# The mean of squares in front of four norms: eight matmul pairs each, or a sum on VectorE and two

## What is computed

```
def rms_norm(x, g):
    xf = x.astype(jnp.float32)
    y = xf * lax.rsqrt(jnp.mean(xf * xf, axis=-1, keepdims=True) + NORM_EPS)
    return (y * g.astype(jnp.float32)).astype(x.dtype)
...
h = h + rms_norm(mixed, W['g_post_mix'][l])
f = rms_norm(h, W['g_pre_ffn'][l]) @ W['w_ffn_in'][l]
f = (jax.nn.silu(f[..., :D_FF]) * f[..., D_FF:]) @ W['w_ffn_out'][l]
h = h + rms_norm(f, W['g_post_ffn'][l])
```

## Time and profile before

| | us |
|---|---|
| median of three runs | 1995.92 |
| the three runs | 1991.81, 1995.92, 2005.24 |
| profiled execution | 2002.46 |
| its span, first to last instruction | 2000.7 |
| TensorE matmul busy | 1829.9 |
| VectorE busy | 790.2 |
| ScalarE busy | 604.3 |
| mean granted clock of TensorE, share of full | 0.954 |

### The profile page before, as it was taken

The page is one execution under the profiler, slowest core; times in us unless marked ns, Lnnn a source line. Parts: engine busy times, 40 slices in busy tenths (PEclk is TensorE's granted clock), DMA queues, the critical chain, the costliest instruction groups (busy, mean ns, idle before and its releaser), DMA issues.

```text
span 2000.7 us, 39700 instructions
## 1 busy us (share of the span) xinstructions
PE 1829.9 (91%) x18348; PEld 1677.0 (84%) x18348; DVE 790.2 (39%) x1122; ACT 604.3 (30%) x992; POOL 22.4 (1%) x37
## 2 busy tenths in 40 slices
PE   7999999879779899999999899677778999999995
PEld 6677789869769799999999799465538999999995
DVE  1556224455541454224432543525123444144422
ACT  4224034323252422122212421344535322222112
POOL 0000000010000000000000000100000000000000
PEclk9999999989969999999999899878988999999998
DMA  8221130001033153464413221241835222333211
GB/s 276 67 80 61 42 96 5 4 16 43 28 117 115 57 184 128 145 224 152 139 59 103 102 92 46 96 139 42 205 80 163 64 78 59 107 85 85 62 55 48
DMA packets 208821, 187.53 MB, mean 94 GB/s; under 512 B 13976, under 2 KB 199448, under 8 KB 207504
## 3 DMA queue, kind: packets, MB, share of 16 engines
q1 hardware_dynamic: 205440, 170.74, 28.0%
q0 software_dynamic: 3216, 14.26, 2.0%
HBM read 170.72 MB, written 41.13 MB: 106 GB/s over the span
## 4 chain that ended last, share of the span: by engine, by line
PE 62%; ACT 3%; DVE 3%; DMA 1%; issue 1%; POOL 0%; DVEq 0%; SPq 0%; POOLq 0%
PE banks L711 49%; PE banks L1246 3%; PE banks L684 2%; PE banks L1016 2%; ACT arena L1498 1%; PE banks L1204 1%; PE banks L1113 1%; PE banks L1173 1%; PE banks L1131 1%; PE banks L1078 0%; DMA out<-arena 0%; POOL out L626 0%; DVE arena_r L2049 0%; DVE arena L2073 0%; ACT arena_r L1632 0%
## 5 line engine op out<-in xcount | busy, mean ns | idle before, releaser
L711 PE MATMUL banks<-arena_r 128*128 128x288 f32 x7440 | 996.5, 296 | 13.3 <-DVE arena_r L2062 13.3
L711 PEld LDWEIGHTS banks<-arena_r 128*128 128x128 f32 x7440 | 990.1, 189 | 16.1 <-issue 13.4
L2049 DVE TENSOR_TENSOR arena_r<-ring,arena_r 128x2048 fp32r<-128x2048 f32 (+2 forms) x84 | 166.8, 1988 | 280.5 <-ACT arena_r L1632 280.5
L670 PE MATMUL banks<-arena,ring 128*128 128x288 f32 (+2 forms) x808 | 199.9, 409 | 0.9 <-ACT mkt L1368 0.7
L1632 ACT ACTIVATE arena_r<-ring 128x2048 fp32r<-128x2048 f32 (+2 forms) x84 | 139.9, 1668 | 195.9 <-PE banks L711 195.8
L670 PEld LDWEIGHTS banks<-arena,ring 128*128 128x128 f32 (+2 forms) x808 | 151.1, 187 | 48.9 <-issue 1.0
L1016 PE MATMUL banks<-consts,arena 128*128 128x128 f32 (+3 forms) x548 | 86.4, 303 | 62.6 <-DMA arena<-in_cache_mem 20.4
L1016 PEld LDWEIGHTS banks<-consts,arena 128*128 128x128 f32 (+3 forms) x548 | 65.6, 157 | 87.0 <-issue 30.1
L838 PE MATMUL banks<-arena 64*64 64x64 f32 x3312 | 112.9, 219 | 8.5 <-DVE arena L1852 3.2
L1322 ACT ACTIVATE arena<-banks 128x576 f32<-128x576 f32 (+1 forms) x77 | 49.8, 648 | 230.1 <-PE banks L670 113.5
L838 PEld LDWEIGHTS banks<-arena 64*64 64x64 f32 x3312 | 105.3, 135 | 12.3 <-DVE arena L1852 3.9
(11 more groups left out here) (217 smaller groups left out, 1416.6 us busy)
## 6 DMA issues: line engine op xcount, KB each, us to landing
ring<-in_w_ffn_in SPq DMA_DIRECT2D x88, 512.0 KB, 5.1
ring<-in_w_ffn_out SPq DMA_DIRECT2D x32, 704.0 KB, 4.6
out<-in_cache_win_g SPq DMA_DIRECT2D x16, 1016.0 KB, 7.4
ring<-in_a_w_in SPq DMA_DIRECT2D x10, 1024.0 KB, 5.0
arena<-in_cache_win_g SPq DMA_DIRECT2D x80, 128.0 KB, 6.7
arena<-in_cache_mem SPq DMA_DIRECT2D x16, 512.0 KB, 4.6
arena<-in_cache_win_g SPq DMA_DIRECT2D x16, 512.0 KB, 6.8
out<-in_cache_win_g SPq DMA_DIRECT2D x8, 1008.0 KB, 7.1
```

Source lines behind the costliest of these rows:

```text
L670: last = mm(banks[0:m, s + a, 0:HALF], w[0:parts, k, c0:c0 + m], x[0:parts, k, a * HALF:(a + 1) * HALF], start=(k == 0), stop=(k == nk - 1))
L711: last = mm(banks[:, s + a, 0:HALF], w[i][:, k, c0:c0 + P], x[j][:, k, a * HALF:(a + 1) * HALF], start=(k == 0 and m == 0), stop=(k == nk ...
L2049: last = v.tensor_tensor(lo, ring[:, n % RING, 0:nk * w], hi.bitcast(F32), ALU.subtract)
```

## The change

For norms 1, 3, 5 and 7 the squares of tiles 0 to 6 are added up by VectorE into one tile, `sq_sum`, which lies in the memory of the recurrent state (no longer used there); tile 0 is squared straight into it. The squares of the other tiles go to the two halves of `gate` in turn. TensorE then runs two pairs for a norm, both behind the last tile: the sum, and tile 7. New semaphores: `sq_made` counts squares, `sq_added` additions, six for a norm. ScalarE's square of tile c waits, from c = 3 on, for the addition of tile c-2, which frees its buffer.

In the mix VectorE's additions stand between its weight subtractions; in the feed-forward the addition for tile c-1 stands behind its add to `y` for tile c and ahead of the weight subtraction. `sq_ready` now counts the squares of the even norms alone.

```
+        sq_sum = state[:, :, :, :].rearrange("p a c v -> p (a c v)")[:, 0:T]
+        def sq_tile(c):
+            return gate[:, c % 2, :] if c else sq_sum
...
+            def mean_of_sums(n):
+                for m, (x, ready, count) in enumerate(((sq_sum, sq_added, KD - 2), (sq_tile(KD - 1), sq_made, KD))):
+                    pe.wait_ge(ready, count * (n // 2 + 1))
+                    for a in range(2):
+                        last = mm(banks[:, 6 + a, 0:HALF], const("mean"), x[:, a * HALF:(a + 1) * HALF], start=(m == 0), stop=(m == 1))
+                last.then_inc(ms_ready, 1)
...
                     project_parts(w, (c % 2) * P, x_parts, nk, new_x if c == 0 else None)
-                    if c >= 2:
-                        mean_square(norm, sq_y, c - 2)
-                for c in range(KD - 2, KD):
-                    mean_square(norm, sq_y, c)
+                mean_of_sums(norm)
...
                         project_parts(take_parts(), 0, f_parts, HF, new_f=None if c else KF * l + half * HF)
-                        if half and c >= 2:
-                            mean_square(norm + 2, sq_f, c - 2)
-                for c in range(KD - 2, KD):
-                    mean_square(norm + 2, sq_f, c)
+                mean_of_sums(norm + 2)
...
+            def square_tile(c, i, src):
+                if c >= 3:
+                    act.wait_ge(sq_added, (KD - 2) * i + c - 2)
+                dst = sq_tile(c)
+                f(dst if src.shape == dst.shape else halves(dst), src, ACT.Square).then_inc(sq_made, 1)
...
-                    f(halves(sq_y[:, c, :]), bankpair(n), ACT.Square).then_inc(sq_ready, 1)
+                    square_tile(c, norm // 2, bankpair(n))
...
-                            square(sq_f, y, c)
+                            square_tile(c, norm // 2 + 1, y[:, c, :])
...
+            def add_squares(c, i):
+                if 1 <= c < KD - 1:
+                    dve.wait_ge(sq_made, KD * i + c + 1)
+                    if c > 1:
+                        dve.wait_ge(sq_added, (KD - 2) * i + c - 1)
+                    v.tensor_tensor(sq_sum, sq_sum, sq_tile(c), ALU.add).then_inc(sq_added, 1)
...
-                for _ in range(4):
-                    low_weights()
+                for c in range(KD):
+                    add_squares(c, norm // 2)
+                    if c % 2:
+                        low_weights()
...
                             v.tensor_tensor(halves(y[:, c, :]), bankpair(n), halves(y[:, c, :]), ALU.add).then_inc(tile_free, 1)
+                            add_squares(c - 1, norm // 2 + 1)
                         low_weights()
```

More of the change, by code:

```diff
@@ L252, in trunk @@
         h = at(A_H, KD, T)
-        sq_y, sq_h, sq_f = at(A_SQY, KD, T), at(A_SQH, KD, T), at(A_XH, KD, T)
+        sq_h = at(A_SQH, KD, T)
         y = at(A_Y, KD, T)
@@ L413, in trunk @@
         sq_ready, ms_ready, rstd_ready = [sem(n) for n in ("sq_ready", "ms_ready", "rstd_ready")]
+        sq_made, sq_added = sem("sq_made"), sem("sq_added")
         xn_ready, xlast_ready, xlast_t, shift_ready = [sem(n) for n in (
@@ L680, in mean_square @@
             def mean_square(n, src, k):
-                pe.wait_ge(sq_ready, KD * n + k + 1)
+                pe.wait_ge(sq_ready, KD * (n // 2) + k + 1)
                 for a in range(2):
@@ L2096, in add_normed, with mix_out @@
                         v.tensor_tensor(h[:, k - 1, :], h[:, k - 1, :], y[:, k - 1, :], ALU.add).then_inc(h_ready, 1)
-            def mix_out(src, nk):
+            def add_squares(c, i):
[4 more added lines that the diff above has]
+                    v.tensor_tensor(sq_sum, sq_sum, sq_tile(c), ALU.add).then_inc(sq_added, 1)
+            def mix_out(norm, src, nk):
                 low_weights()
@@ L2128, in feed_forward @@
                             v.tensor_tensor(halves(y[:, c, :]), bankpair(n), halves(y[:, c, :]), ALU.add).then_inc(tile_free, 1)
+                            add_squares(c - 1, norm // 2 + 1)
                         low_weights()
             dve.wait_ge(h_back, 16)
-            mix_out(att[0]["cat"], KD)
+            mix_out(1, att[0]["cat"], KD)
             feed_forward(0, 1)
@@ L2162, in _ @@
             last_split[0] = len(split_at)
-            mix_out(att[1]["cat"], 4)
+            mix_out(5, att[1]["cat"], 4)
             dve.wait_ge(h_back, 32)
```

## The result

Four runs of the changed kernel have a median of 1970.45 us (1961.54 to 1984.11), four of the kernel before 1993.87 us (1990.26 to 2005.24). The ratio is 0.9877, with an interval of 0.9829 to 0.9925: faster by 0.75 to 1.71%, so clear of no change, but not of the 1% at which the forecast split its chances. Forecast were 1977.5 us and a range of 1968 to 1989. The profiled execution took 1975.83 us, its span is 1974.0.

The account below looks back on a forecast made before the run. TensorE, busy 91% of the span, was taken to set the time between tiles. Removed pairs 19.2 us less norm 7's tail 0.8 give 18.4 us, from 1995.92 to 1977.5 us; range 1968 to 1989.

Parts of the forecast that it names:

- The price of a pair between tiles: On TensorE, a mean-square pair between two tiles costs 0.96 us, bounds 0.75 and 1.10, from 9.77 against 8.81 us.
- (b): Rival: pairs only filled time while the next tile's weights were made, tiles keep their period; 1995 us, chance 0.04.
- Five pairs of a stage, not six: In four stages only five removed pairs lie between TensorE's tiles: 4 x 5 x 0.96 = 19.2 us saved, bounds 15.0 to 22.0.
- (a): Rival: the tails count as well, all 24 removed pairs at 0.96 save 23.0 us; 1972.9 us, chance 0.07.
- Norm 7's tail: Behind the last feed-forward tile the sum's pair waits for VectorE, delaying the logarithm: +0.8 us, from -0.1 to +1.9.
- The additions at nothing: Twenty-four VectorE additions of 0.75 us, all but the last beside TensorE's tiles, cost nothing; without cover 18 us together.
- (d): Rival: additions in VectorE's queue hold up the weights, from 4.2 us of added delay per tile; +74, 2070 us, chance 0.02.
- (c): Clock rival: longer gaps behind norms 1 and 5 slow each TensorE restart by 0.66 us; 1.3 us, 1979, chance 0.05.
- The sum: Whole kernel: 19.2 - 0.8 = 18.4 us saved, from the median 1995.92 to 1977.5 us, a gain of 0.92%; chance 0.82.

Follow-up runs that it names:

- the repeats: Both kernels run again with no edit: the changed kernel 0.9881 against the kernel before, median of its six runs 1983.64 us; the kernel before 2001.98 us.
- the two halves: The change for norms 3 and 7 alone (feed-forward), 0.9951, and for norms 1 and 5 alone (mix), 0.9962, each against the kernel before.

## Why the prediction held, point by point

- **The price of a pair between tiles**, 0.96 us. The pair put back measured 0.96, and the tiles of the changed kernel take 8.58 or 8.80 us instead of 9.77; so (b), by which the tile would keep its period, did not come about. Right, with a condition that the trace of the kernel before already showed and I didn't see (rows in the last section): in a stream at the quicker pace the tile is 8.58, and a pair then costs 9.76 - 8.58 = 1.18 us. The reason given for 0.96, that it holds the change-over between the two kinds of matmul too, isn't borne out: one, two and three pairs in a row take 1.13, 2.10 and 3.07 us, so a further pair without a change-over costs 0.97 as well.
- **Five pairs of a stage, not six.** In the repeats without a change of pace the stages shrank by 5.9, 4.8, 4.7 and 5.0 us, and by 4.8, 4.8, 4.8 and 4.0 with their starts taken out. The tails of norms 1, 3 and 5 gave nothing back: the logarithm of norm 5 starts 4.5 us after its last tile as before (1498.97 to 1503.47), that of norm 3 6.2 (1075.83 to 1082.01). So (a) did not come about.
- **Norm 7's tail**, +0.8. Forecast were 3.9 us from the last tile, measured 3.9; the earlier addition, which takes away only the wait, makes it 3.0, 0.1 below the kernel before, the lower bound of this term. Its upper bound, +1.9, is 2.1 by its own rows (1972.90 + 2.10 - 1972.94); the forecast doesn't hang on it.
- **The additions at nothing.** Twenty-four of 0.754 us moved no tile, nor did three more for each of those in the feed-forwards, and in the trace of the change ScalarE waits for no addition. (d) fell as far as it was tried: it was to decide from 4.2 us of added delay a tile, and the experiment gave 2.3.
- **The clock** (c). Behind norms 1 and 5 the gap grew by 0.94 us (7.40 to 8.34 and 7.47 to 8.41), as forecast, and no cost of it can be made out. In nine profiles with the same first three tiles, these take 28.5 to 29.9 us behind six gaps of the one length and 28.4 to 29.9 behind twelve of the other, on average 29.3 and 29.1. The 5.0 us of the last stage in the repeats, where 4.0 were due, hold 1.0 us of this scatter. The Trainium skill (TensorE: Matmul & The Clock Gate, section "Why this matters for your kernels") warns of idle gaps between bursts of matmuls, behind which the clock is back at its half. Here the clock falls in these gaps before and after the change (0.50 at every restart), so that rule gives no price for a gap that grows from 7.4 to 8.4 us, and (c) read more into it than it says. What a late burst can cost shows in the run with four additions, where the second pair of a tail took 2.13 us instead of 1.13.
- **The sum.** 18.4 us. Measured: 24.5 and 23.8 by the two ratios, 23.4 and 18.8 by the medians, 19.4 and 20.3 by the touched stages, 18.4 by those of the repeats with their starts taken out, 17.4 by the two halves. The mechanism is shown by the stages; that both medians, 1970.45 and 1983.64, lie in the range is in part luck and in part its width, for runs of one kernel lie over 20 us apart. The chances (0.57 for within 1%, 0.40 for faster) were right to split there: 1% lies inside both intervals of the change, 0.9829 to 0.9925 and 0.9844 to 0.9917. That the ratios came out at 1.2% rather than 0.9% can't be settled below the scatter of the untouched stages and the two paces.

## What to carry to other kernels

Small matmuls between the tiles of a busy TensorE cost their whole time, here 0.96 us a pair: read the price from the same stage with and without them, and count only those that lie between tiles. Work that joins several results can go to an engine with room (here VectorE, busy 39% of the span), but see which wait ends last behind the final tile: one line decided whether the sum was ready when the last tile ended or 1.5 us too late. Where stages differ between two profiles by more than the effect, take the difference stage by stage before explaining the total.

## What was not expected: two paces of the same stream

The long streams of split matmuls run at one of two paces, at a granted clock of 1.00 in either: 96 matmuls in 12.48 us (130.0 ns each) or in 12.80 us (133.3 ns each). A stream keeps its pace from behind the first three tiles of a feed-forward (whose groups with a pair take 3.36 us at either pace) to its end or its next pair, over some 400 us. Of 20 feed-forwards in ten profiles two ran at 12.48: the second in the first profile of before and the first in the first profile of after; repeats of the same kernels had 12.80 there. A stretch from restart to restart took 434.1 us at the one pace and 445.2 at the other, so one stream is worth some 11 us, about half of the effect of this change. In that first profile of before the tiles took 8.58 us up to the first pair and 9.75 to 9.77 from there on, as in all streams with pairs. VectorE's adds of four tiles there, the last two with a pair between them:

```profile
1904.07 0.76 DVE L2128 TENSOR_TENSOR arena<-banks,arena 128x576 f32<-128x576 f32 x1 [4.32 <-PE banks L711]
...
1912.64 0.76 DVE L2128 TENSOR_TENSOR arena<-banks,arena 128x576 f32<-128x576 f32 x1 [4.11 <-PE banks L711]
...
1921.22 0.76 DVE L2128 TENSOR_TENSOR arena<-banks,arena 128x576 f32<-128x576 f32 x1 [4.17 <-PE banks L711]
...
1930.97 0.76 DVE L2128 TENSOR_TENSOR arena<-banks,arena 128x576 f32<-128x576 f32 x1 [5.35 <-PE banks L711]
```

This looks as if a pair ended the quicker pace, which fits 8.80 + 0.96, but no run here isolates it. What sets the pace at the start stays open.
